# HGRN's preparation moved between the outputs of the projections of the even layer

## The reference

```python
q, i, f_fwd, f_bwd, g = cols                 # five of the projections u @ w_in
q = silu(q); v = i
f = lb + (1.0 - lb) * sigmoid(fp)            # per direction
k, lf = 1.0 - f, log(f)
# hgrn2_scan, per chunk of 32 tokens, per direction
a_cum = cumsum(lf)                           # within the chunk; a_end its last, a_mid its middle value
s_loc = (k * exp(a_end - a_cum)).T @ v
s_in  = running state:  s = exp(a_end) * s + s_loc
inter = (q * exp(a_cum)) @ s_in
sc    = tril((q * exp(a_cum - a_mid)) @ (k * exp(a_mid - a_cum)).T)
out   = inter + sc @ v
```

## Time and profile before

| what | us |
|---|---|
| median of 3 runs (2287.85 to 2296.91) | 2288.52 |
| the profiled execution | 2285.25 |
| its span | 2283.4 |
| TensorE busy in the span | 1906.7 |
| VectorE busy | 854.3 |
| ScalarE busy | 271.2 |

### The profile page before, as it was taken

The page is one execution under the profiler, slowest core; times in us unless marked ns, Lnnn a source line. Parts: engine busy times, 40 slices in busy tenths (PEclk is TensorE's granted clock), DMA queues, the critical chain, the costliest instruction groups (busy, mean ns, idle before and its releaser), DMA issues. The chain is left out here.

```text
span 2283.4 us, 31808 instructions
## 1 busy us (share of the span) xinstructions
PE 1906.7 (84%) x10720; PEld 980.5 (43%) x10721; DVE 854.3 (37%) x1780; ACT 271.2 (12%) x549; POOL 654.7 (29%) x947
## 2 busy tenths in 40 slices
PE   6999994487689979999996788596689878877894
PEld 2334442354545534555553343244455444433442
DVE  0224446855623322333331827443343222222224
ACT  2122223212100000000001110101100000000001
POOL 0000000000256645666662000000056444444440
PEclk9999997799799999999998989798789999998997
DMA  8565410050379999989992670314369999999934
GB/s 349 219 235 208 186 37 1 1 212 28 157 273 410 411 415 411 388 344 412 387 412 114 255 276 30 147 37 161 134 261 409 412 414 413 412 413 410 408 138 202
DMA packets 99830, 601.66 MB, mean 263 GB/s; under 512 B 23232, under 2 KB 23339, under 8 KB 40300
## 3 DMA queue, kind: packets, MB, share of 16 engines
q1 hardware_dynamic: 64540, 499.67, 54.0%
q0 software_dynamic: 35216, 100.98, 11.8%
HBM read 590.50 MB, written 51.92 MB: 281 GB/s over the span
## 5 line engine op out<-in xcount | busy, mean ns | idle before, releaser
L1717 PE MATMUL bank<-moe_w,blk_xT 128*64 128x256 f32 x5632 | 682.0, 397 | 0.0
L1717 PEld LDWEIGHTS bank<-moe_w,blk_xT 128*64 128x64 f32 x5632 | 405.6, 142 | 219.2 <-issue 32.4
L1728 PE MATMUL bank<-moe_w,xt 128*64 128x512 f32 x1408 | 332.1, 592 | 1.5 <-DVE xt L1805 1.5
L1644 POOL DMA_INDIRECT ada_rows<-v_tokens,blk_gidx x264 | 272.5, 1032 | 140.4 <-issue 135.0
L1793 DVE STREAM_TRANSPOSE blk_xT<-ada_rows 128x512 f32<-128x512 f32 x132 | 94.0, 712 | 451.4 <-PE bank L1717 431.1
L492 PE MATMUL bank<-moe_w,xt 128*128 128x512 f32 x544 | 243.6, 605 | 12.7 <-DMA moe_w<-in_odd_w_in 9.9
L1660 POOL DMA_INDIRECT y_rows<-xt,blk_sidx x176 | 180.0, 1023 | 96.8 <-issue 48.4
L1812 DVE COPY xt<-bank 128x512 f32<-128x512 f32 x176 | 121.8, 692 | 149.3 <-PE bank L1728 149.3
L1776 ACT ACTIVATE xt<-bank 128x128 f32<-128x128 f32 x174 | 48.3, 278 | 1057.6 <-PE bank L1717 1057.6
L492 PEld LDWEIGHTS bank<-moe_w,xt 128*128 128x128 f32 x544 | 103.2, 193 | 147.0 <-issue 135.9
L1728 PEld LDWEIGHTS bank<-moe_w,xt 128*64 128x64 f32 x1408 | 100.9, 137 | 127.5 <-issue 100.5
(11 more groups left out here) (373 smaller groups left out, 1635.3 us busy)
## 6 DMA issues: line engine op xcount, KB each, us to landing
moe_w<-in_experts SPq DMA_DIRECT2D x128, 3072.0 KB, 34.2
moe_w<-in_ada_w POOLq DMA_DIRECT2D x20, 2048.0 KB, 8.3
moe_w<-y_rows SPq DMA_DIRECT2D x24, 1024.0 KB, 19.7
moe_w<-in_even_w_in SPq DMA_DIRECT2D x8, 2048.0 KB, 8.9
moe_w<-in_odd_w_in SPq DMA_DIRECT2D x7, 2048.0 KB, 12.3
moe_w<-in_ada_w SPq DMA_DIRECT2D x4, 2048.0 KB, 14.3
ada_rows<-v_tokens,blk_gidx POOLq DMA_INDIRECT x264
moe_w<-in_even_w_out SPq DMA_DIRECT2D x1, 4096.0 KB, 14.0
```

Of the source, the lines that this page charges most:

```text
L1644: pool.indirect_dma_start(came[q][:, u], None, v_quarters, bass.IndirectOffsetOnAxis(ap=gidx[q][:, u:u + 1], axis=0), bounds_check=4 * n_t ...
L1717: last = nc.tensor.matmul(g.bank[1][64 * h:64 * h + 64, 0:HID], xT[:, k], w[:, s, (2 * k + h) * HID:(2 * k + h + 1) * HID], start=k == 0, ...
L1728: last = nc.tensor.matmul(g.bank[3][64 * h:64 * h + 64, :], hT[:, 64 * m:64 * m + 64], w[:, s, at:at + 512], start=m == 0, stop=m == 1)
```

## The change

- The preparation of both directions leaves the HGRN stage. It is spread over slots 17 to 31 of the projection stage (`prepare` on VectorE, `prepare_act` on ScalarE), direction 0 by the table `(21, 22, 23, 24, 25, 26, 27)`, direction 1 by `(25, ..., 31)`. The affine step goes from VectorE to ScalarE, one instruction for each output, a slot after it.
- It computes in place and in the mLSTM's own arrays once these are done with (exponentials in `qkT`, `v1`, `e`, `o`), in `mod_row` and in half of the room of the adaLN ring.
- The order of the projection's groups becomes mLSTM q/k, v, o, HGRN q, ff, fb, then i and g.
- `PER_HEAD` is 4 instead of 5, `ADA_STEPS` begin at 1, 5, 9, 13, 17 instead of 2, 7, 12, 17, 22. There is one y buffer and one adaLN row buffer instead of two of each; the adaLN copy of ScalarE stands at step 4 of its group, not at step 3.
- TensorE's side work is partly put in the middle of an output (`pe_mid`, between its fourth and fifth matmul).
- The HGRN stage is one block: eight tiles, both directions one behind the other. The state ring has 9 slots in one array, and at the turn of the direction four memsets put zero where the last four updates were.
- The lower bounds are loaded by POOL ahead of the gate weights, with two memsets of `reset`, instead of by SP in the HGRN stage.

The core of the diff. The first two lines are in `projection_stage`, in TensorE's list; the copy with `at + 4` is in ScalarE's list of `EvenSide`, the loop over `floor, scan, ...` in VectorE's; what follows it is in `hgrn_stage`:

```diff
+                        if side and k == KT // 2:
+                            side.pe_mid(pe, n)
-    BANKS, TAIL = 2, 1
+    BANKS, TAIL = 2, 0
-    ADA_STEPS = (2, 7, 12, 17, 22)
-    HEAD0, PER_HEAD = 8, 5
+    ADA_STEPS = (1, 5, 9, 13, 17)
+    HEAD0, PER_HEAD = 8, 4
+    AFFINE = {17 + j: (0, j) for j in range(HEADS)} | {21 + j: (1, j) for j in range(HEADS)}
...
+    def pe_mid(self, pe, n):
+        for i, at in enumerate(self.ADA_STEPS):
+            if at <= n < at + 4:
+                self.ada.multiply(pe, 4 * i + n - at)
+        h, a = self.head_step(n)
+        if a == 0 and 1 <= h <= HEADS:
+            self.values(pe, h - 1, 1)
+        if a == 2 and 0 <= h < HEADS:
+            self.scores(pe, h, 1)
+        if a == 3 and 0 <= h < HEADS:
+            self.values(pe, h, 0)
...
-            if n == at + 3:
+            if n == at + 4:
                 self.ada.copy(act, i)
...
+        for d, (floor, scan, centre, end, q1, q2, by_k) in enumerate(((21, 22, 23, 24, 25, 26, 27), (25, 26, 27, 28, 29, 30, 31))):
...
+            if n == floor:
+                dve.wait_ge(self.affine, HEADS * (d + 1))
...
+                for half in halves:
+                    link(nc.vector.tensor_scalar(u["k"][:, half], A[:, half], -1.0, 1.0, ALU.mult, ALU.add))
+                link(nc.vector.tensor_scalar(A[:, halves[0]], A[:, halves[0]], TINY, None, ALU.max))
+                nc.vector.tensor_scalar(A[:, halves[1]], A[:, halves[1]], TINY, None, ALU.max).then_inc(self.floored, 1)
+            if n == scan:
...
+                for h in range(HEADS):
+                    dve.wait_ge(self.logged, 2 * d + h // 2 + 1)
...
-            tiles = [0, 1, 2, 3] if d == 0 else [1, 0, 3, 2]
-            chunk_order = list(range(TILE_CH)) if d == 0 else list(range(TILE_CH))[::-1]
+    seq = [(0, i) for i in (0, 1, 2, 3)] + [(1, i) for i in (1, 0, 3, 2)]
+    order = [list(range(TILE_CH)), list(range(TILE_CH))[::-1]]
...
+                            if n == NT - 1 and m == TILE_CH - 1:
+                                nc.vector.memset(state(h, gc + 1), 0.0).then_inc(stated, 1)
+                                continue
```

More of the change, by code:

```diff
@@ L766, in dve @@
                 self.finish(dve, h - 1, 0)
-        if a == 1 and own:
-            self.weigh(dve, h, 0, 0)
-            self.clamp(dve, h, 1)
+        if a == 1:
+            if own:
+                self.clamp(dve, h, 1)
+                self.weigh(dve, h, 0, 0)
+            if old:
+                self.finish(dve, h - 1, 1)
+                self.norm_sums(h - 1)
         if a == 2:
@@ L1902, in even_layer @@
[L1902 to L1907 removed]
+            sb3 = lambda shape: g.arena.bottom(c3, shape)
@@ new lines, in even_layer, with _ @@
+            s["prep"] = [{"k": late[:, 1, 0], "K1": flat(ff), "D1": late[:, 1, 1], "Q1": flat(qkT), "Q2": flat(e[:, 0]), "dend": dend[:, 0]},
+                         {"k": flat(g.mod_row), "K1": flat(fb), "D1": flat(e[:, 1]), "Q1": v1.rearrange("p i h c -> p (i h c)")[:, 0:2048], "Q2": flat(o),
+                          "dend": dend[:, 1]}]
+            ones = new_sem(g, "v_ones")
+            with ExitStack() as c4:
+                with nc.Block() as block:
+                    @block.gpsimd
+                    def _(pool):
+                        pool.memset(v1[:, :, :, P:P + 1], 1.0).then_inc(ones, 1)
+                        pool.wait_ge(ones, 1)
+                w_in = InputWeights(g, c4, g.dram["even_w_in"], [0, 1, 2, 3, 5, 6, 4, 7], 2)
+                modulate_stage(g, 0, 0, 1, allt, None, w_in)
+                rows = [flat(x) for x in (g.mix, q, v)]
+                room = {"B": rows[0][:, 0:2 * T], "a": rows[0][:, 2 * T:4 * T], "m": rows[0][:, 4 * T:6 * T], "ones": rows[0][:, 6 * T:8 * T],
+                        "x": rows[1][:, 0:2 * T], "e": rows[1][:, 2 * T:4 * T], "lf": rows[2][:, 0:2 * T]}
+                projection_stage(g, g.dram["even_w_in"], [
+                    (0, "T", allt, lambda j: (qT if j < 2 else kT)[:, j % 2], "q_scale"),
+                    (1, "N", allt, lambda j: v1[:, j, :, 0:P], "heads"),
+                    (2, "N", allt, lambda j: o[:, j], "sigmoid"),
+                    (3, "T", allt, lambda j: q[:, j], "silu"),
+                    (5, "T", allt, lambda j: ff[:, j], "sigmoid"),
+                    (6, "T", allt, lambda j: fb[:, j], "sigmoid"),
+                    (4, "N", allt, lambda j: v[:, j], "copy"),
+                    (7, "N", allt, lambda j: hg[:, j], "silu")],
+                    lambda ctx: EvenSide(g, ctx, s, room, [late[:, i].rearrange("p a c -> p (a c)") for i in range(2)]), prefetched=w_in)
```

513 lines of the change are left out of this document (249 added, 264 removed).

## The result

| | before | after |
|---|---|---|
| median of the runs, us | 2288.18 (4 runs) | 2259.32 (4 runs, 2257.79 to 2261.66) |
| ratio | 1 | 0.9869, 95% interval 0.984 to 0.9899 |
| profiled execution: time, span, us | 2285.25, 2283.4 | 2257.79, 2256.0 |
| mean granted clock | 0.926 | 0.928 |

The change makes the kernel 1.3% faster: 28.9 us by the medians, 27.5 by the profiled executions. Forecast were 42.6 us and 2246, with 2257 as the slow end of the range. The direction was right; a third of the gain is missing.

The account below looks back on a forecast made before the run. TensorE paces the projection stage, with VectorE alone in two HGRN stretches: -55.4 for preparation, -8.0 for scans, +20.8 of projection costs make -42.6 us, so 2246 us; eight-in-ten range 2237 to 2257.

Parts of the forecast that it names:

- The stretches without TensorE: HGRN stage: two preparation stretches of 29.30 and 26.10 us with TensorE at nothing go, -55.4 us.
- (b): Projection stage, slot 22: TensorE waits 4.7 us for VectorE before the scores of head 3; none at heads 1 and 2.
- the rival with contention: VectorE's memory-wide operations, moved beside TensorE and DMA, are slowed; at 2.5 times their time 2301 us; chance 0.04.
- a late direction 1: Rival: direction 1's preparation ends behind the last output and the scans wait: 12.4 us, time 2258; chance 0.06.
- smaller waits: Rival: TensorE's waits for head 3's scores and in slots 25 to 27 vanish: 7.9 us less, 2238; chance 0.09.
- (a): Projection stage: TensorE's transposes wait for ScalarE's adaLN copy at four outputs, 3.1 us each, 12.4 in all.
- or the clock falling at the long waits: Half of a rival: projection waits half as long again, through VectorE or the clock; 9 to 11 us more, 2256; chance 0.15.
- The two pieces of an output: Projection stage: cutting outputs in two for work between costs nothing, as matmul kinds already changed twice in a slot.
- GpSimd's memset: Scans: POOL's memset of `sc`, 2.38 us of work, is done before the first local states, 2.7 us in.

Follow-up runs that it names:

- the kernel before with the late copy: Kernel before with one edit: ScalarE copies the adaLN rows one slot later, the preparation staying in its own stage; 2319.6 us, ratio 1.012.

## Why the prediction was wrong

*Right.* The stretches without TensorE went, -55.4. All waits stand where they were forecast and have nearly the forecast sizes; (b)'s 4.7 shows as 4.50 once the stop ahead of it is gone. Direction 1 was ready in time. The wide operations of VectorE weren't slowed: the scans over 128 x 512 took 1223 ns beside TensorE, 1224 alone. So the rival with contention fell, and those with a late direction 1 and with smaller waits too.

*The step that failed* is the one put as "by the rows (a) is free and (b) costs 0 to 2.2". Measured, (a) and (b) together cost 12.2 us of clock beside 14.8 of waiting, 2.4 us a stop. The working had one row for "3 us of standing still costs nothing": eight transposes in 1.09 us after 3.45. The Trainium skill ("TensorE: Matmul & The Clock Gate", section "HAM oscillation — how this bites in real kernels") describes a fall to the low clock at every wait, in a kernel whose matmuls come in bursts between DMA waits of about 3 to 5 us. This trace agrees, at its five stops of 2.81 to 3.00 us; other runs here have the fall behind shorter stops, too. By that rule, with the 2.2 us of the earlier trace rows a stop, the prediction had 11 us and 2257. That the time came out at 2259 is in part luck: the shorter waits and the rest of the program gave back 4.0 us, the longer pieces and the slower matmuls behind the stage took 6.7. The rule was set aside for a row, and the row was a draw of a coin. In the 14 traces of this case the same eight transposes after the same 3.45 us took 1.09 or 1.10 eight times and 1.97 six times. The scans' stop of 3.03 us cost nothing in both places of the before trace, and 1.5 to 4.0 us at 10 of the 15 places of all traces (from the local states of the second tile to those of the third, 5.68 us at full clock). And the earlier trace rows has more in it than I took: it is about what a few small transposes do next, not eight wide matmuls at full pace.

The rival "or the clock falling at the long waits" gave 2256, and its second half was the right one; both halves together had 0.15. The rows had more for it: TensorE at 1.00 for 308 us had no stop in it at all, so the trace of before didn't show what a stop in that stage does. That was an unknown with bounds of 0 and, by 2.2 a stop, 11; I took the lower end and should have kept both.

*Smaller misses:* The two pieces of an output "cost nothing in my sum"; they and the rest of the order took about 2 us. The sum had no term for the scans' 3.0 us and the norm's 1.4, both slower matmuls after stops that the trace of before had too. GpSimd's memset did hold VectorE up by 1.24 us, against the forecast, but the scores that VectorE needs next would have held it up for 1.03 of them.

What stays open: why the first output of the stage took from 7.11 to 10.21 us in these traces, why half outputs of 5.40 us stand now and then behind no stop, and why the stops of 1.68 to 2.10 us at the end of the projection stage cost nothing. The first two move a trace by 2 to 5 us, and explain why totals agree less well than places.

## What to carry to other kernels

In a stage where TensorE runs at full pace, price a stop of about 3 us at its length plus about as much again (2.4 us a stop in the changed kernel, 3.8 in the kernel before with the late copy), and treat "the clock stays up" as proven only by several places, not by one row. Before moving work beside such a stage, look where each wait of TensorE would end, and put the piece that it waits for (here four small copies on ScalarE) ahead of the long one in its engine's queue: that one line was worth 0.7 to 0.9% of this kernel's time. Where a stop can't be moved, give TensorE real work of its length; matmuls of no use win back the clock, not the wait.

## What the runs showed of the hardware

Stops of TensorE between outputs, over all traces: 17 of 3.0 us on the copy had slow matmuls behind them, 17 of 17; five of 2.81 to 4.51 us on the scores of head 3, five of five; six of 1.27 to 2.13 us, six of six; nine of 0.4 us and ten of 0.94 to 1.06 us, none. The place counts as well as the length. Between the last output and the first turn of keys TensorE stands still for 1.68 to 2.10 us in eleven traces, and in all of them the turns, scores and local states behind it ran at full pace (0.63, 1.06 and 1.17 us behind 1.75 in the changed kernel).

In the scans, where TensorE is busy in short pieces, a stop of 3.03 us brought the clock down at 10 of 15 places with the same instructions around it. How much was lost didn't follow the stop's length: 1.7 us behind 1.27 and behind 2.81, and behind four stops of 3.00 in one trace 3.4, 1.8, 3.4 and 1.9.
